# Gathered expert rows taken earlier in a two-layer step, with the slots, the one-hot chunks and one key search moved in the hand-written order

## The chip, the cores and the metric

The kernel runs on one core of a Trainium2 chip, as one launch. The metric is the device time of one execution in microseconds (us), less is better. The engines are TensorE (PE in the profile, PEld for its weight loads), VectorE (DVE), ScalarE (ACT), GpSimd (POOL) and the issuing engine SyncE (SP).

## The reference, cut to what matters

The step has DEPTH = 2 layers over 128 prompt tokens (tile 0) and 512 latent tokens (tiles 1 to 4). Each layer has an attention and gating part and then PEER, a retrieval of experts, which is where the changed code lies:

```python
q = (x @ w_q).reshape(n, PEER_HEADS, 2, PEER_HALF)          # 8 heads
s1 = jnp.einsum('nhd,kd->nhk', q[:, :, 0], key1)            # 128 keys each
s2 = jnp.einsum('nhd,kd->nhk', q[:, :, 1], key2)
t1, i1 = lax.top_k(s1, 16); t2, i2 = lax.top_k(s2, 16)
cand = t1[..., :, None] + t2[..., None, :]
top, pos = lax.top_k(cand.reshape(n, 8, 256), 16)           # 128 experts a token
g = jax.nn.softmax(top, axis=-1)
a = jnp.einsum('thkd,td->thk', u_tab[ib], xb)
w = jax.nn.gelu(a) * gb
out = jnp.einsum('thk,thkd->td', w, v_tab[ib])              # tables of 16384 x 1024
```

Everything is float32.

## The kernel before, in words

**Two ways to do the experts.** A token needs 128 rows of `peer_u` and 128 of `peer_v`. A tile can be *gathered*: POOL issues one indirect DMA for each of 128 slots (each brings one row of 1024 numbers for each of the 128 tokens, 512 KB), DVE multiplies and sums (`dot_rows`, line 1313, for u; `add_rows`, line 1331, for v). Or it can be *dense*: PE multiplies by the whole table, 128 blocks of 128 experts, and most products get a weight of zero. Tiles 0 and 2 are gathered in both halves, tiles 3 and 4 are dense in both, and tile 1 is gathered for u and dense for v (`GATHERED`, `U_DENSE`, `V_DENSE`). "A row" below is one such slot of a tile, written u0, v0, u1, u2, v2 by table and tile; each of the five has 128.

**The stages of a layer.** First the *front*, once for the prompt (g = "P") and once for the latent tiles (g = "S"): input projection, attention, output projection, query projection with the scores of the keys, and the first tile's key search. Then the *u pass* (line 942): PE runs 128 blocks, each 8 matmuls (16 instructions in the profile) over 256 tokens. Then the *v pass* (line 970): 128 blocks of 12 instructions, each over 512 columns, for three tiles. `u_order` writes the order of PE and ACT in the u pass by hand. Between the blocks stand, for each tile k of `V_DENSE` = [3, 4, 1], one slot job `slT` (line 947: the chosen experts' numbers and weights are transposed) after the block that `SLOT_BLOCKS` names, and then 32 chunks `g` (line 954), after the blocks that `chunk_block` names. A chunk turns one-hot vectors of four tokens into their gate weights over all experts.

**DVE has one order of its own**, written out at the end of `build`: the searches (`choosing(k, i)`: i = 0 to 15 are the sixteen half-key searches, done in pairs on odd i; i = 16 to 21 combine them), the one-hots of a chunk (`one_hots`, lines 1499 and 1504, at most 5 chunks ahead of PE), and rows between them. `slots_out(k)` tells PE that slT may run; `one_hots(k, 0)` waits until ACT has emptied slT's bank. Then comes the v pass, where `weights_T(b)` (line 1514) makes the weights of block b, at most four blocks ahead of PE, with the rows of tiles 0 and 2 between. Blocks up to `LAST_U` have the last v0 rows and the rest of tile 2's search, then `finish_gathered(0)`; those up to `LAST_V` have the u2 rows, those up to `LAST_END` the v2 rows.

**Rows come through a ring of GP = 8 buffers.** POOL issues them in the order of `ROWS` (line 681) as DVE releases buffers, so a row that DVE takes later is also loaded later. In the front, DVE takes u0 rows with `prompt_rows(n)`: some before the attention, one or two beside each of its 32 heads, 8 after it, some before and beside the queries; `expert_weights(0)` then needs the Gelu of ACT over all 128 dots (`gelu_dots(0)`, which waits for the last u0 row), and `add_rows(0, ...)` begins.

**SP and ACT issue the other transfers**: SP the blocks of both tables (two blocks a DMA, four DMAs ahead), the stores of the u pass's activations and half of the gate stores, and their loads in the v pass (`load_gates`, `load_acts`); ACT the other half of the gate stores. ACT also runs in order, and waits in it for DVE at `top_softmax(k)` and `gelu_dots(k)`, which stand at written blocks.

## Time and profile before

| | |
|---|---|
| median of 3 runs | 3688.99 us (3688.4 to 3696.15) |
| the profiled execution's own time | 3688.44 us |
| its span in the profile | 3686.3 us |
| PE busy | 3445.9 us (93%) |
| DVE busy | 2621.7 us (71%) |
| ACT busy, POOL busy | 861.4 us (23%), 1602.0 us (43%) |
| moved by DMA | 1263.48 MB, mean 343 GB/s |
| mean granted TensorE clock | 0.966 |

The page gives busy times over the whole span, and PE looks full. The matmul ends are modelled, though, so for PE the number of instructions in a stretch beside its length says more than the busy time. The two layers are alike, and a layer's stages have different limits, so a stretch has to be read by itself.

### The profile page before, as it was taken

The page shows a single profiled execution, that of the slowest core. Times are in us where ns is not written, and L with a number is a line of the kernel's source. Part 1 is how long each engine was busy: PE and PEld are TensorE (multiplying, and loading weights), DVE is VectorE, ACT ScalarE, POOL GpSimd, SP SyncE. Part 2 cuts the span into 40 slices and gives each one's busy share as a digit, 9 for nine tenths or more (in the row PEclk, how much of TensorE's full clock was granted, in tenths as well). Part 3 has the DMA queues.
Part 4 walks back from the last instruction along what each step waited for, and adds up shares of the span by engine and source line. Part 5 has one row for each costly group of instructions (what it writes and reads, how often), then busy time and mean ns, then how long its engine had stood idle before and what let it go on. Part 6 is the DMA issues. An engine that isn't in the chain of part 4 may idle for free.

```text
span 3686.3 us, 38219 instructions
## 1 busy us (share of the span) xinstructions
PE 3445.9 (93%) x12478; PEld 2100.3 (57%) x12478; DVE 2621.7 (71%) x6009; ACT 861.4 (23%) x2206; POOL 1602.0 (43%) x1362
## 2 busy tenths in 40 slices
PE   6898989999799999999988988999998999999998
PEld 2555446889687444444435554488986864444443
DVE  0377786978788766666645786789787886666667
ACT  1115211158632000000021260111685210000000
POOL 2044265424642555555400542645156235555552
PEclk9898999999999999999989989999998999999999
DMA  9866588999999999999974864899899999999994
GB/s 361 331 241 218 181 322 328 380 325 345 409 406 367 397 384 414 414 413 413 374 268 151 311 202 173 329 365 402 292 386 409 397 357 386 414 414 413 414 413 193
DMA packets 413988, 1263.48 MB, mean 343 GB/s; under 512 B 36240, under 2 KB 139664, under 8 KB 370784
## 3 DMA queue, kind: packets, MB, share of 16 engines
q0 software_dynamic: 192000, 721.61, 50.5%
q1 hardware_dynamic: 171808, 514.20, 36.8%
q10 hardware_dynamic: 49984, 25.23, 2.3%
q8 instruction: 101, 1.65, 0.2%
q14 instruction: 95, 0.78, 0.1%
HBM read 1174.07 MB, written 86.84 MB: 342 GB/s over the span
## 4 chain that ended last, share of the span: by engine, by line
PE 52%; DMA 27%; DVE 8%; issue 5%; POOL 4%; ACT 2%; SPq 1%; ACTq 0%; DVEq 0%; POOLq 0%
PE P L942 21%; DMA ring<-in_peer_v_dram,eidx 12%; DMA ring<-in_peer_u_dram,eidx 10%; PE P L916 8%; POOL ring L681 4%; PE T L954 4%; PE P L750 4%; PE P L767 4%; DMA ring<-in_w_mod_dram 2%; PE P L970 2%; PE O L814 2%; PE T L750 2%; DMA gate_d<-area 1%; DVE ring L1313 1%; DVE late L1331 1%
## 5 line engine op out<-in xcount | busy, mean ns | idle before, releaser
L681 POOL DMA_INDIRECT ring<-in_peer_u_dram,eidx x768 | 947.1, 1233 | 1139.6 <-DVE ring L1313 785.9
L1313 DVE SCALAR_TENSOR_TENSOR ring<-ring,h 128x1024 f32<-128x1024 f32 x768 | 925.0, 1223 | 296.9 <-DMA ring<-in_peer_u_dram,eidx 289.8
L970 PE MATMUL P<-w_ring,area 128*128 128x512 f32 x2048 | 927.3, 596 | 33.9 <-DVE area L1514 32.4
L942 PE MATMUL P<-hT,w_ring 128*128 128x256 f32 x4096 | 921.1, 383 | 0.0
L681 POOL DMA_INDIRECT ring<-in_peer_v_dram,eidx x512 | 615.1, 1201 | 671.7 <-DVE late L1331 347.0
L942 PEld LDWEIGHTS P<-hT,w_ring 128*128 128x128 f32 x4096 | 778.4, 193 | 102.8
L970 PEld LDWEIGHTS P<-w_ring,area 128*128 128x128 f32 x2048 | 388.7, 191 | 535.2 <-issue 535.2
L1331 DVE SCALAR_TENSOR_TENSOR h<-ring,dots,h 128x1024 f32<-128x1024 f32 x254 | 325.9, 1283 | 184.5 <-DMA ring<-in_peer_v_dram,eidx 175.8
L1331 DVE SCALAR_TENSOR_TENSOR late<-ring,dots,late 128x1024 f32<-128x1024 f32 x254 | 325.8, 1283 | 71.3 <-DMA ring<-in_peer_v_dram,eidx 56.3
L916 PE MATMUL P<-hT,w_ring 128*128 128x128 f32 (+1 forms) x1024 | 286.4, 441 | 2.9 <-issue 2.9
L970 PE MATMUL O<-w_ring,qT 128*128 128x512 f32 x512 | 261.4, 592 | 0.0
L970 PE MATMUL V<-w_ring,qT 128*128 128x512 f32 x512 | 261.4, 592 | 0.0
L916 PEld LDWEIGHTS P<-hT,w_ring 128*128 128x128 f32 x1024 | 158.2, 195 | 127.1 <-issue 122.7
L1199 ACT ACTIVATE qT<-hT 128x128 f32<-128x128 f32 x128 | 39.3, 309 | 625.6 <-PE V L970 625.6
L1199 ACT ACTIVATE qT<-area 128x128 f32<-128x128 f32 x128 | 38.9, 309 | 586.6 <-PE V L970 586.6
L970 PEld LDWEIGHTS O<-w_ring,qT 128*128 128x128 f32 x512 | 97.3, 190 | 122.7 <-issue 122.7
L970 PEld LDWEIGHTS V<-w_ring,qT 128*128 128x128 f32 x512 | 97.3, 190 | 122.5 <-issue 122.5
L954 PE MATMUL T<-row 128*128 128x128 f32 x912 | 126.4, 287 | 35.4 <-issue 33.9
L954 PEld LDWEIGHTS T<-row 128*128 128x128 f32 x912 | 120.6, 200 | 45.5 <-issue 39.1
L750 PE MATMUL P<-w_ring,hT 128*128 128x512 f32 x320 | 142.2, 604 | 3.0 <-ACT hT L1088 3.0
L767 PE MATMUL P<-w_ring,hT 128*128 128x512 f32 x320 | 139.1, 593 | 1.5 <-issue 1.5
L647 POOL DMA_DIRECT2D ring<-in_w_mod_dram x48 | 25.8, 540 | 207.2 <-PE O L717 146.8
(233 smaller groups left out, 3205.0 us busy)
## 6 DMA issues: line engine op xcount, KB each, us to landing
w_ring<-in_peer_uT_dram SPq DMA_DIRECT2D x128, 1024.0 KB, 8.3
w_ring<-in_peer_vB_dram SPq DMA_DIRECT2D x128, 1024.0 KB, 8.2
ring<-in_w_mod_dram POOLq DMA_DIRECT2D x48, 1024.0 KB, 8.3
w_ring<-in_peer_wq_dram SPq DMA_DIRECT2D x64, 512.0 KB, 5.8
h<-acts_d SPq DMA_DIRECT2D x64, 512.0 KB, 9.0
w_ring<-in_w_in_dram SPq DMA_DIRECT2D x48, 512.0 KB, 5.0
area<-gate_d SPq DMA_DIRECT2D x16, 1536.0 KB, 14.2
hT<-gate_d SPq DMA_DIRECT2D x16, 1536.0 KB, 14.4
```

The lines of the kernel that those rows point to most:

```text
L647: pool.dma_start(m_slots[:, u % MR], chunks(w_mod)[ml, :, c, n * MW:(n + 1) * MW]).then_inc(m_full[u % MR], 16)
L681: pool.indirect_dma_start(out=ring[:, b, :], out_offset=None, in_=tables["uv".index(phase)], in_offset=bass.IndirectOffsetOnAxis(ap=eidx[: ...
L750: mm = pe.matmul(out[:, 0:width], hT[:, c, t * P:(t + 1) * P], w[:, c % 2, 0:width], start=c == 0, stop=c == DC - 1)
L767: mm = pe.matmul(out[:, :], hT[:, c, t * P:(t + 1) * P], w_ring[:, ws[4 * n + q], c % 2, :], start=c == 0, stop=c == DC - 1)
L814: mm = pe.matmul(out[:, :], v_pad[:, kb, HD * kv:HD * kv + P], pT[:, kv, i, :], start=kv == 0 and i == 0, stop=kv == 1 and i == len(keyb) - 1)
L916: mm = pe.matmul(out[:, 0:nt * P], w[:, c % 2, j * P:(j + 1) * P], hT[:, c, 0:nt * P], start=c == 0, stop=c == DC - 1)
L942: mm = pe.matmul(out[:, 0:TOKENS], w[:, c * P:(c + 1) * P], hT[:, c, TOKENS:2 * TOKENS], start=c == 0, stop=c == DC - 1)
L954: mm = pe.matmul(out[:, j * P:(j + 1) * P], oh_b[n % OH_BUFS][:, j, :], oh_a[n % OH_BUFS][:, j, :], start=True, stop=True)
L970: mm = pe.matmul(bank[ACC[2 * t + half]][:, :], w, uv_ring[:, b // 2 % (WR // 2), b % 2, half * 512:(half + 1) * 512], start=b == 0, stop= ...
L1199: act.activation(wdot_T[:, b % 4, :].rearrange("p (s t) -> p s t", t=SUB), gate_in[b // 8 % 2][:, ACT_SUBS:SUBS, b % 8, :], ACT.Copy).then ...
L1313: dve.scalar_tensor_tensor(ring[:, b, :], ring[:, b, :], 1.0, h2[:, k, :], ALU.mult, ALU.mult, accum_out=dots[:, k, row:row + 1]).then_inc ...
L1331: dve.scalar_tensor_tensor(acc[k], ring[:, b, :], dots[:, k, row:row + 1], acc[k], ALU.mult, ALU.add).then_inc(row_used[b], 1)
```

## The change

It keeps every operation and every byte, and changes only where they stand in the order. In the front of the latent tiles, 36 u0 rows instead of 28 stand before the attention, two after each of the first three tiles of the output projection, 18 instead of 24 before the queries, 20 instead of 28 beside the first queries. ACT's Gelu of the dots comes at query 7 instead of 10, and 52 v0 rows instead of 40 lie beside queries 7 to 15. In the u pass the first search (tile 3) has 20 v0 rows (24 before) and 16 u1 rows, the search of tile 4 has 32 u1 rows (16 before), the chunks of tile 4 have 62 u1 rows (78 before) and the sixteen half-key searches of tile 2, which stood at the end of the pass; the chunks of tile 1 have 28 v0 rows (16 before). Slots come after blocks 43, 75 and 101 (50, 78 and 103 before), chunks from block 47, 77 and 103 (52, 80 and 105). In the v pass 28 v0 rows are left (48 before), tile 2's u rows lie at blocks 14 to 69 (20 to 70), its v rows at 70 to 122 (71 to 122).

```diff
-PV_EARLY = 64
-PV_LATE = 80
+PV_EARLY = 72
+IN_ROWS = 36
+OUT_ROWS = 2
+QUERY_ROWS = 52
+PV_LATE = 100
...
-LAST_U = 20
-LAST_V = 71
+LAST_U = 14
+LAST_V = 70
...
-SLOT_BLOCKS = {50: 3, 78: 4, 103: 1}
+SLOT_BLOCKS = {43: 3, 75: 4, 101: 1}
 
 SEARCH_CHUNKS = 22
 
+ROWS_BESIDE = 32
...
     if k == 3:
-        return 52 + q if q < SEARCH_CHUNKS else 73 + (q - SEARCH_CHUNKS) // 2
-    first, blocks = {4: (80, 23), 1: (105, 16)}[k]
+        return 47 + q if q < SEARCH_CHUNKS else 70 + (q - SEARCH_CHUNKS) // 2
+    first, blocks = {4: (77, 23), 1: (103, 16)}[k]
...
-                        if g == "S" and j == 10:
+                        if g == "S" and j == 7:
                             gelu_dots(0)
...
-                        if b == 43:
+                        if b == 41:
                             top_softmax(3)
-                        if b == 68:
+                        if b == 65:
                             top_softmax(4)
-                        if b == 102:
+                        if b == 100:
                             gelu_dots(1)
...
                     if latent:
-                        prompt_rows(28)
+                        prompt_rows(IN_ROWS)
...
                         norm_modulate(g, t)
+                        if latent and t < nt - 1:
+                            prompt_rows(OUT_ROWS)
                     if latent:
-                        prompt_rows(SLOTS - 28 - 40 - GP - 28)
+                        prompt_rows(SLOTS - IN_ROWS - 40 - GP - OUT_ROWS * (nt - 1) - 20)
                     modulation("summed")
                     for j in range(2 * PH):
-                        if latent and j < 8:
-                            prompt_rows(3 + j % 2)
-                        if latent and j == 10:
+                        if latent and j < 5:
+                            prompt_rows(4)
+                        if latent and j == 7:
                             expert_weights(0)
-                        if latent and j >= 10:
-                            add_rows(0, 40 * (j - 10) // 6, 40 * (j - 9) // 6)
+                        if latent and j >= 7:
+                            add_rows(0, QUERY_ROWS * (j - 7) // 9, QUERY_ROWS * (j - 6) // 9)
                         first_tile_keys(g, j)
...
                 for i in range(2 * PH + 6):
                     if i < 12:
-                        add_rows(0, 40 + 2 * i, 42 + 2 * i)
+                        add_rows(0, QUERY_ROWS + (PV_EARLY - QUERY_ROWS) * i // 12,
+                                 QUERY_ROWS + (PV_EARLY - QUERY_ROWS) * (i + 1) // 12)
...
                 for i in range(2 * PH + 6):
-                    dot_rows(1, 16 + 16 * i // 22, 16 + 16 * (i + 1) // 22)
+                    dot_rows(1, 16 + ROWS_BESIDE * i // 22, 16 + ROWS_BESIDE * (i + 1) // 22)
                     one_hots(3, i)
                     choosing(4, i)
...
-                    dot_rows(1, 32 + i, 33 + i)
-                dot_rows(1, 42, 50)
+                    dot_rows(1, 16 + ROWS_BESIDE + i, 17 + ROWS_BESIDE + i)
+                near = 16 + ROWS_BESIDE + CHUNKS - SEARCH_CHUNKS + GP
+                dot_rows(1, near - GP, near)
                 for i in range(CHUNKS):
                     one_hots(4, i)
-                    dot_rows(1, 50 + 78 * i // CHUNKS, 50 + 78 * (i + 1) // CHUNKS)
+                    dot_rows(1, near + (SLOTS - near) * i // CHUNKS, near + (SLOTS - near) * (i + 1) // CHUNKS)
+                    if i % 2:
+                        choosing(2, i // 2)
                 slots_out(1)
                 for i in range(CHUNKS):
                     one_hots(1, i)
-                    add_rows(0, PV_EARLY + i // 2, PV_EARLY + (i + 1) // 2)
-
-                for i in range(SEARCHED_EARLY):
-                    choosing(2, i)
+                    add_rows(0, PV_EARLY + (PV_LATE - PV_EARLY) * i // CHUNKS,
+                             PV_EARLY + (PV_LATE - PV_EARLY) * (i + 1) // CHUNKS)
+
                 for b in range(KEYS):
                     weights_T(b)
```

## Rows read from the trace of the kernel before

**Rows 1.** The page: PE's busy time, and GB/s in 40 slices of the span

```profile
PE 3445.9 (93%) x12478; PEld 2100.3 (57%) x12478; DVE 2621.7 (71%) x6009; ACT 861.4 (23%) x2206; POOL 1602.0 (43%) x1362
GB/s 361 331 241 218 181 322 328 380 325 345 409 406 367 397 384 414 414 413 413 374 268 151 311 202 173 329 365 402 292 386 409 397 357 386 414 414 413 414 413 193
```

**Rows 2.** Busy time by stretch, layer 0: length, engines (instructions), clock, DMA share, GB/s

```profile
603.90:780.50 176.60, 176.60 (x822) 155.47 (x821) 145.70 (x422) 25.86 (x59) 78.43 (x65) 1.00 0.97 381
780.50:905.70 125.20, 125.05 (x701) 113.21 (x701) 108.51 (x352) 99.31 (x257) 37.57 (x33) 1.00 0.93 317
905.70:1062.00 156.30, 129.81 (x668) 113.40 (x667) 121.84 (x224) 96.05 (x253) 98.13 (x80) 0.92 1.04 408
1062.00:1175.50 113.50, 111.89 (x642) 101.30 (x641) 94.82 (x309) 27.79 (x61) 19.45 (x18) 1.00 1.03 371
```

**Rows 3.** The same by pass: u and v of layer 0, v of layer 1

```profile
603.90:1175.50 571.60, 543.35 (x2827) 483.39 (x2826) 470.88 (x1307) 249.01 (x628) 233.58 (x194) 0.98 0.99 372
1175.50:1855.00 679.50, 665.37 (x1535) 291.57 (x1536) 464.13 (x706) 41.77 (x131) 354.56 (x303) 0.99 0.99 396
...
2987.60:3669.90 682.30, 663.97 (x1535) 291.61 (x1536) 468.08 (x713) 41.81 (x131) 357.75 (x296) 0.99 0.96 386
```

**Rows 4.** The chain that ended last, in order of time: start, us, what

```profile
402.93 27.47 PE P L767 x64
...
604.04 176.12 PE P L942 x816
...
804.78 0.89 PE T L954 x8
```

**Rows 5.** DMA issues by line: KB each, median us to landing

```profile
w_ring<-in_peer_uT_dram SPq DMA_DIRECT2D x128, 1024.0 KB, 8.3
...
acts_d<-late SPq DMA_DIRECT2D x64, 256.0 KB, 9.9
gate_d<-area ACTq DMA_DIRECT2D x32, 512.0 KB, 13.3
```

**Rows 6.** Waits of PE, and of DVE, between 905 and 1062 us

```profile
PE T L954 <- issue: 26.3, 14, 3.9
...
DVE ring L1313 <- DMA ring<-in_peer_u_dram,eidx: 30.8, 31, 2.7
```

**Rows 7.** Groups of DVE instructions, 907 to 1059 and 1062 to 1141 us

```profile
L1313 DVE SCALAR_TENSOR_TENSOR ring<-ring,h 128x1024 f32<-128x1024 f32 x77 | 93.5, 1222 | 31.4 <-DMA ring<-in_peer_u_dram,eidx 30.3
...
L1331 DVE SCALAR_TENSOR_TENSOR late<-ring,dots,late 128x1024 f32<-128x1024 f32 x16 | 20.4, 1274 | 0.0
```

**Rows 8.** DVE's timeline at the entry of the latent attention, layer 0

```profile
246.48 1.23 DVE L1313 SCALAR_TENSOR_TENSOR ring<-ring,h 128x1024 f32<-128x1024 f32 x1 [0.55 <-DMA ring<-in_peer_u_dram,eidx]
...
278.45 0.61 DVE L1616 CUSTOM_DVE_ANT_0 probs<-P,mask,sink 128x384 f32<-128x384 f32 x1
...
287.55 0.69 DVE L1578 BATCH_NORM_STATS2 stats<-area 128x6 f32<-128x512 f32 x1 [4.22 <-ACT area L1014]
...
296.17 1.22 DVE L1313 SCALAR_TENSOR_TENSOR ring<-ring,h 128x1024 f32<-128x1024 f32 x1
```

**Rows 9.** DVE's timeline in the output projection

```profile
430.51 0.69 DVE L1645 TENSOR_TENSOR tmp<-P,area 128x512 f32<-128x512 f32 x1 [2.03 <-PE P L767]
```

**Rows 10.** DVE's waits between 472 and 604 us

```profile
DVE best L1340 <- ACT key_ring L1127: 22.4, 4, 10.6
```

**Rows 11.** DVE's timeline: one pair of half-key searches between rows

```profile
616.15 0.48 DVE L1340 MAX8 best<-key_ring 128x8 f32<-128x128 f32 x2
...
618.62 8.23 DVE L1331 SCALAR_TENSOR_TENSOR late<-ring,dots,late 128x1024 f32<-128x1024 f32 x6
```

**Rows 12.** DVE's timeline: end of tile 1's search, first one-hots of tile 3

```profile
670.87 0.23 DVE L1450 TENSOR_SCALAR eidx<-tmp 128x128 uint32<-128x128 f32 x1
...
781.22 0.69 DVE L1499 TENSOR_TENSOR h<-qT,cst 128x512 f32<-128x512 f32 x1 [13.78 <-ACT qT L1170]
```

**Rows 13.** PE's timeline after `finish_gathered(0)`

```profile
1293.30 6.70 PE L970 MATMUL P<-w_ring,area 128*128 128x512 f32 x8 [6.08 <-DVE area L1514]
```

## The prediction, on record before the changed kernel was built

> **What bounds the kernel now.** I read the page first. It has PE busy for 93% of the span, and it has the transfers near one ceiling, 406 to 414 GB/s, in most slices of the two passes [rows 1]. Neither says which of the two ends a stage, so I went to the stages.
>
> The chain of waits gives what PE needs when nothing holds it: 51 blocks of the u pass in 176.12 us, 3.454 us a block; a chunk in 0.89 us; and 64 instructions over 512 columns in 27.47 us, 0.4292 us each, so 12 x 0.4292 = 5.15 us for a block of the v pass [rows 4]. The u pass needs 128 x 3.454 + 96 x 0.887 = 527 us and took 571.6: **44 us of stall**. The v pass needs 659.4 us and took 679.5 in layer 0 and 682.3 in layer 1: **20 and 23 us** [rows 3]. Nothing else in these two passes can be won, and the fronts, 1181 us or so of the span for both layers, hold the rest.
>
> The stretches of the u pass show where the 44 us lie [rows 2]. Up to 780.5 and 905.7 us PE runs at its floor while the transfers leave room (381 and 317 GB/s). From 905.7 to 1062 us they are full at 408 GB/s, and PE does 25 blocks and 32 chunks, 114.8 us of work, in 156.3 us: 41.5 of the 44. There DVE waited 30.8 us for u rows and PE 26.3 us in 14 waits before chunks [rows 6]. The rest is the clock, granted at 0.92 of 2.4 GHz there and at 1.00 in the stretch before. So 78 rows, packed between the chunks of tile 4, are too many for the transfers, DVE comes late with the one-hots, and PE waits.
>
> **The change, part by part.** A row moves 128 x 1024 x 4 = 0.524 MB, a u block 0.524, its activations 0.131, a chunk's gates 0.262 MB [rows 5, 7]. Positions below are for layer 0 in the times of the old trace; layer 1 repeats them.
>
> *Projection, +8 rows.* DVE took 19 rows in 246.48 to 278.45, 1.68 us each, as it waited for them to land; eight more are 13.4 us. It has cover: after three heads it waited for ACT's Gelu until 287.55 [rows 8], and further between tiles. But ACT's Gelu stands behind the first two heads' Exp, so it moves with DVE: heads at 291.9, Gelu done about 299, the statistics' end at 302.3 in place of 296.17. From there the heads run through DVE, ACT and PE in turn, and I see nothing that catches up. **+6.0 us** a layer; the ends are 0 (all absorbed by waits between tiles) and +13.4.
>
> *Output projection, +6 rows.* Two rows are 2.3 us, and in each tile DVE waits for the second half of PE's product, 2.0 us in the smallest case [rows 9]; before the queries there are 6 rows fewer. 0; without that cover 3 x 2.3 = 7 us.
>
> *Queries.* From the last LayerNorm on DVE has 18 + 20 + 52 = 90 rows, before 24 + 28 + 40 = 92. It still waits for the keys' copies (22.4 us before [rows 10]), but fewer rows are left where the u pass begins and its blocks load beside them. My estimate: 2 rows are 2.6 us, and as much again from those that needn't land in that crowd, so tile 1's search ends near 665 us instead of 670.87 [rows 12]; the ends are 659 and 675 (four rows more in that part, five more us of waits). ACT's Gelu of the dots at query 7 needs row u0 127: 38 rows at 1.22 to 1.68 us and two pair searches, 51 to 69 us [rows 7, 8, 11], against two groups of queries of 27.47 us and their keys, some 61 us. 0 to +8 us; I take 0, since these rows wait in the ring when the part begins and the ring refills during each search.
>
> *First slots.* DVE had finished tile 3's slots 13.78 us before ACT emptied them [rows 12]. The new place is 7 blocks, 24.2 us, earlier: 603.9 + 44 x 3.454 = 755.9 us. DVE started this part 6 us earlier and has 36 instead of 40 rows in it (-5 us): 767.4 - 6 - 5 = 756.4. It fits to a microsecond, and each microsecond that DVE is later is one that PE waits.
>
> *Search of tile 4, up to its slots.* 32 blocks and 32 chunks are 138.9 us of PE. 50 rows, blocks, activations and gates are 55.6 MB, 400 GB/s: just under the ceiling. So slots 4 at 895 us, against 905.7, with three blocks fewer done.
>
> *Chunks of tile 4.* 26 blocks and 32 chunks are 118.2 us of PE. Transfers: 17.0 + 8.4 + 62 x 0.524 = 57.9 MB; the same count gives 65.7 for the old stretch, which moved 408 x 156.3 = 63.8, so I take off 2 to 3.5: 54.4 / 0.408 = 134 us. DVE was busy 121.84 us [rows 2]; 16 rows less at 1.22 and eight pair searches at 2.47 more [rows 7, 11] leave 122. So 134 us, transfers still the limit: the stall falls from 41.5 to 16.
>
> *Chunks of tile 1 and the end.* 26 blocks and 32 chunks, 118.2 us. DVE was busy 94.82 us there [rows 2]; 12 v0 rows more are 15.3 and the searches gone 19.8 us. The last chunk comes two blocks earlier, so the last gate store, on which SP's loads for the v pass wait, has more cover. No stall.
>
> Sum for the u pass: 152 + 139 + 134 + 118.2 + 4 for slots and gaps = 547; I add 5 because two stretches now run within 3% of the transfers' ceiling and DVE meets its first slot without reserve: 552 us, **-19.5 us**. The ends: 0 (bytes of the pass unchanged, and if its stretches don't level out nothing is won) and -26 (no allowance, and less at the ceiling).
>
> *V pass.* It loses 20 rows: 304 were left and 284 are. It moved 396 x 679.5 = 269 MB; now 258.6, 392 GB/s at PE's floor. Blocks 2 to 19 had 48 rows, 2.67 each; now blocks 2 to 13 have 28, 2.33. That matters at `finish_gathered(0)`: DVE came to it without lead and PE waited 6.08 us, then ran 8 instructions at twice their time, +3.4 us [rows 13]. DVE's work from block 2 falls from 3.85 to 3.45 us a block beside the search, against PE's 5.15; the search's 22 us are in both. I expect the 9.5 us gone, and half of the other 11 us, since the u2 rows thin out from 2.51 to 2.29 a block but v2 rows only from 2.46 to 2.42: **-12.5 us** (0 to -18).
>
> Nothing of the kernel's end moves. Sum: 2 x (6.0 - 19.5 - 12.5) = -52. Of this I keep -49, since the first layer's and the second's front can each lose the microsecond or two of ACT's Gelu: 3688.4 - 49 = **3639 us**, against the profiled execution's own 3688.44, which stands 0.5 us under the median 3688.99 and so can be set for it.
>
> **The rivals.** *A, the deadlines win.* DVE misses the earlier slot. It decides if DVE comes to tile 3's slots at or after 767 us in old times, that is, if the query part gives nothing back. For it: the forecast has no reserve there, and the slots moved 24 us while DVE had 13.8. The price: 11 us at the first slots, 5 at tile 4's, DVE and transfers in series in tile 4's chunks (122 busy + 28 of waits as before = 150 instead of 134 us), so the u pass takes 552 + 11 + 5 + 16 = 584, +12 us; with +6 in the front and -8 in the v pass that is +10 a layer: **3708 us**. Against it: the rows before the slots become fewer. *B, half.* The stretch at 400 GB/s stalls too, u pass -9, v pass -9, front +7: -11 a layer, **3666 us**. For it: at 408 GB/s PE stalled in the old trace, and the step from 400 is small. *C, more.* The attention absorbs the late start between its tiles, and the passes reach their floors: 0 - 25 - 17 = -42 a layer, **3605 us**. *D, nothing.* The transfers can't be held above the u pass's mean: its 372 x 571.6 = 212.6 MB take 571 us again, wherever they stand, and the front's +6 meets -6 in the v pass: **3688 us**. Against it: 408 GB/s over 156 us, and 396 over the v pass [rows 2, 3]. The Trainium skill ("DMA: Bandwidth & Descriptors", "Where 436 GB/s comes from") says that between HBM and SBUF the memory's share of a core, about 358 GB/s, binds; by it the u pass would need 594 us and filling light stretches would win nothing. The rows just named lie above that figure, so the trace doesn't agree.
>
> **How the numbers follow.** Forecast 0.50 (its own range 3624 to 3655), A 0.09, B 0.23, C 0.12, D 0.06. The range reaches into B, D and C: 3612 to 3684. Faster by over 0.2% (7 us, about what a measurement can tell from no change): forecast, B, C and the upper part of D, 0.86. Within: 0.05. Slower: 0.09.
>
> **What the profile would show.** Right: the statistics of the latent attention end about 6 us later after its start; DVE's wait at tile 3's first one-hots is a few us instead of 13.8; the stretch of tile 4's search moves 380 to 400 GB/s instead of 317; PE's waits before chunks fall from 26 to some 10 us; the u pass takes 546 to 558 us; PE doesn't wait for line 1514 after `finish_gathered(0)`; the v pass takes 665 to 670 us. Wrong: PE idle before tile 3's slots, ACT waiting for DVE at `gelu_dots(0)` with PE behind it, or a u pass still above 565 us.

## The result, and the profile after

The changed kernel takes **3666.17 us** in the median of 4 runs (3659.94 to 3672.84); the kernel before, run beside it, 3689.59 us (3688.4 to 3696.15). The ratio is 0.993, with the 95% interval 0.9917 to 0.9944. A second set of runs gave it 3653.24 us against 3692.92, ratio 0.9886 (0.9872 to 0.9901). So it is faster by 0.7 to 1.1%, inside the range given and 27 us (in the second set 14) above the forecast of 3639. The two sets' intervals don't overlap, so a difference of some 10 us between kernels of different sets says little. The profiled execution took 3659.94 us, with a span of 3658.1, 28.2 less than before; the second set's profile has the same span.

The page of the changed kernel, the lines that answer to [rows 1]:

```profile
PE 3434.4 (94%) x12478; PEld 2101.6 (57%) x12478; DVE 2617.4 (72%) x6009; ACT 860.4 (24%) x2206; POOL 1728.9 (47%) x1362
...
GB/s 361 329 225 264 197 308 326 379 370 370 408 387 377 390 414 413 399 414 412 333 273 153 340 205 194 306 390 375 360 382 408 349 383 401 413 414 398 413 415 170
```

The transfers are more level, as intended, and PE is as full as it was. The page says no more. (Lines of the changed kernel are 5 higher than before: 942 is 947, 1313 is 1318, 1514 is 1519, and so on; x2 and x4 add 2, e3 adds 1.) The changed kernel by stretch, in the columns of [rows 2]: the u pass of layer 0 cut at the Gelus of blocks 43, 75 and 101, then the v passes of both layers.

```profile
610.80:762.80 152.00, 152.00 (x705) 133.47 (x703) 136.87 (x412) 23.10 (x52) 69.24 (x58) 1.00 0.98 386
762.80:908.20 145.40, 141.29 (x775) 127.67 (x775) 130.69 (x392) 101.96 (x262) 68.88 (x51) 0.99 1.00 365
908.20:1058.70 150.50, 127.11 (x678) 112.49 (x677) 120.03 (x320) 93.58 (x254) 82.93 (x65) 0.94 1.05 406
1058.70:1178.10 119.40, 118.67 (x676) 107.61 (x674) 86.75 (x191) 30.27 (x63) 56.11 (x28) 1.00 1.01 369
1178.10:1838.90 660.80, 659.30 (x1536) 291.53 (x1537) 443.54 (x688) 42.18 (x131) 363.29 (x283) 1.00 0.98 392
...
2982.60:3641.80 659.20, 659.14 (x1535) 291.56 (x1536) 445.49 (x692) 42.23 (x131) 357.72 (x276) 1.00 0.95 383
```

[Rows 2] were cut where the kernel before has its stages. For a like comparison the kernel before is cut at the same blocks, 43 to 75 to 101 to 127:

```profile
756.00:893.20 137.20, 137.12 (x744) 123.55 (x744) 110.33 (x353) 96.73 (x247) 33.19 (x30) 1.00 0.91 310
893.20:1051.80 158.60, 132.93 (x687) 116.44 (x685) 122.68 (x223) 101.95 (x269) 102.70 (x81) 0.92 1.04 408
1051.80:1175.50 123.70, 121.20 (x692) 109.48 (x692) 103.36 (x327) 30.28 (x66) 24.98 (x23) 1.00 1.03 374
```

From here A is blocks 0 to 43, B 44 to 75, C 76 to 101 with the chunks of tile 4, D 102 to 127 with the chunks of tile 1 (in the old placement the slots and chunks stand a few blocks later). With [rows 4] the changed kernel's PE needs 152, 138.9, 118.2 and 118.2 us in them, and 659.4 us in the v pass; the shortest that any run with this placement shows are 139.4 us for B and 119.4 for D. Every profile, cut so:

```
us                layer 0:  A     B     C     D     v     u    layer 1:  B     C     D     v     u
before                    152.1 137.1 158.7 123.7 679.5 571.6          137.1 158.8 123.1 682.3 571.2
after                     152.1 145.3 150.5 119.4 660.8 567.3          147.9 151.4 125.3 659.2 576.6
after, second set         152.1 147.7 150.7 119.4 658.8 569.9          147.5 151.0 119.4 659.7 570.0
e1 old slots, chunks      152.1 137.1 158.1 124.1 660.6 571.4          137.1 158.5 124.0 659.5 571.7
e2 28 rows first          152.1 145.4 150.8 119.4 658.8 567.7          147.9 150.8 119.4 659.7 570.2
e3 half of a u block      152.1 139.4 137.8 119.4 658.8 548.7          139.4 138.3 119.4 659.7 549.2
e4 gates stored early     152.1 144.1 150.2 119.4 658.8 565.8          148.5 149.2 119.4 659.5 569.2
e5 16 rows back into C    152.1 148.4 161.8 122.9 660.9 585.2          147.6 163.3 120.0 661.0 582.9
e6 20 v0 rows back        152.1 148.5 150.6 119.4 677.5 570.6          141.5 150.7 119.5 679.7 563.8
e7 before, gates early    152.1 137.1 159.6 128.8 677.3 577.7          137.1 159.8 127.8 680.9 576.9
e8 before, new front      152.1 137.1 158.8 123.6 679.2 571.7          137.1 158.8 124.7 683.6 572.7
x1 slots 2 blocks later   152.1 139.4 149.7 126.2 658.8 567.4          139.4 148.2 126.2 659.7 565.9
x2 v0 rows held back      152.1 145.0 149.7 122.2 658.8 569.1          141.4 150.1 120.1 659.6 563.6
x4 x2 and e4              152.1 147.6 144.2 119.9 660.5 563.8          145.7 145.3 119.4 659.7 562.6
```

The 28.2 us of span split into -16.2 in layer 0 (fronts +6.8, u pass -4.3, v pass -18.7) and -12 in layer 1 (+5.8, +5.4, -23.1). **The v pass brought all of it, and more; the u pass, meant to bring most, brought little.** The second set's profile has it 1.7 and 1.2 us shorter than before.

*V pass.* It is at PE's floor. Before, in layer 0, PE waited 14.1 us in 14 waits for the weights of line 1514. In the changed kernel there are two short waits for them (line 1519 now). DVE, which before had waited 197 us for rows in this pass and never for PE's blocks, now waits 56 us for rows and 139.5 us for PE to catch up, four blocks behind it. Then DVE's timeline around `finish_gathered(0)`, which answers to [rows 13]; PE doesn't stop there:

```profile
PE P L975 <- DVE area L1519: 2.2, 2, 1.5
...
DVE area L1519 <- PE V L975: 139.5, 83, 4.7
```

```profile
1245.45 1.22 DVE L1310 TENSOR_TENSOR late<-late,h 128x1024 f32<-128x1024 f32 x1
...
1254.27 1.22 DVE L1318 SCALAR_TENSOR_TENSOR ring<-ring,h 128x1024 f32<-128x1024 f32 x1
```

*Front.* DVE's timeline in layer 0: entry of the latent attention and the first row after the statistics there, against [rows 8]; end of tile 1's search, tile 3's slots ready, and first one-hots of tile 3, against [rows 12]. Then PE's first use of tile 3's slots.

```profile
293.32 0.61 DVE L1621 CUSTOM_DVE_ANT_0 probs<-P,mask,sink 128x384 f32<-128x384 f32 x1
...
305.36 1.22 DVE L1318 SCALAR_TENSOR_TENSOR ring<-ring,h 128x1024 f32<-128x1024 f32 x1
...
679.10 0.23 DVE L1455 TENSOR_SCALAR eidx<-tmp 128x128 uint32<-128x128 f32 x1
...
766.42 0.29 DVE L1448 TENSOR_TENSOR gsm<-gsm,gsum 128x128 f32<-128x128 f32 x1
...
768.52 0.69 DVE L1504 TENSOR_TENSOR h<-qT,cst 128x512 f32<-128x512 f32 x1 [0.42 <-ACT qT L1175]
```

```profile
766.92 0.66 PE L952 MATMUL O<-ident,r 128*128 128x128 f32 x2 [4.11 <-DVEq L1491]
```

The attention begins 14.9 us later and its statistics end 9.2 us later (305.36 against 296.17). Of both, 3.4 us already stand ahead of the changed code, where tile 0's search ends at 215.2 us instead of 211.8. Counted from there the statistics end 5.8 us later, and 7.4 in layer 1, about as forecast, and the latent front up to the u pass is 3.4 and 6.5 us longer. But tile 1's search ends 68.3 us after the u pass begins (610.8), not earlier than before (67.0 after 603.9). DVE still waits for the keys' copies:

```profile
DVE best L1345 <- ACT key_ring L1132: 24.8, 2, 16.4
```

*Stretch B.* PE's only wait in it, and the 3.4 us behind that wait:

```profile
PE O L952 <- DVEq L1491: 4.1, 1, 4.1
```

```profile
766.90:770.30 3.40, 3.38 (x10) 2.86 (x11) 2.98 (x5) 2.41 (x7) 2.77 (x2) 0.52 0.92 309
```

PE waits 4.1 us for tile 3's slots, and then runs at a granted clock of 0.52, near the lower level of 1.2 GHz. Its busy time in B is 141.3 us against 139.4 in a run without that wait (x1 below). So 4.1 and 1.9 make the 6 us by which B is over that. In layer 1 the wait is 5.6 us and B 147.9: 8.5 over, 5.6 and 2.9. No transfer holds PE up in B, and DVE waits there 0.8 us for rows.

*Stretch C.* Waits of the changed kernel between 908.2 and 1058.7 us (who, for whom: sum, count, longest). [Rows 6] had DVE waiting for rows, and PE before chunks without a releaser that the profile names; a chunk can wait for its one-hots.

```profile
ACT area L1190 <- DMA gate_d<-area: 24.2, 3, 9.4
DVE dots L1295 <- ACT dots L1079: 18.1, 1, 18.1
...
PE T L959 <- ACT area L1190: 11.7, 5, 7.1
...
ACT hT L1190 <- DMA gate_d<-hT: 11.2, 2, 6.1
...
PE T L959 <- ACT hT L1190: 7.7, 3, 4.9
DVE ring L1318 <- DMA ring<-in_peer_u_dram,eidx: 7.5, 7, 1.9
...
PE T L959 <- issue: 3.9, 1, 3.9
```

Now PE waits for ACT to empty a chunk's bank, and ACT for the gate stores to land and give their buffers back. DVE's waits for rows are down from 30.8 to 7.5 us, and at the end of C DVE stands 18.1 us ahead, waiting for ACT's Gelu of tile 1's dots. The forecast had foreseen the fall in DVE's waits, not ACT's part. PE's three waits sum to 23.3 of the 32.3 us by which C is over 118.2; the other 9 are PE busy for 127.1 us, at a granted clock of 0.94 in the stretch.

### The profile page after: what moved, and what is told of

Read it like the earlier page. It is cut to its first block, busy times and chain, and to the rows that moved or that the text cites. A ratio compares the mean times of both kernels' runs of the same rounds, so it can differ in the third digit from the quotient of the medians.

```text
span 3658.1 us, 38233 instructions
## 1 busy us (share of the span) xinstructions
PE 3434.4 (94%) x12478; PEld 2101.6 (57%) x12478; DVE 2617.4 (72%) x6009; ACT 860.4 (24%) x2206; POOL 1728.9 (47%) x1362
## 4 chain that ended last, share of the span: by engine, by line
PE 66%; DVE 14%; DMA 11%; issue 3%; POOL 2%; ACT 2%; SPq 1%; ACTq 0%; DVEq 0%; POOLq 0%
PE P L975 23%; PE P L947 10%; PE P L921 6%; PE V L975 6%; PE O L975 6%; DVE late L1336 4%; PE P L772 4%; DMA gate_d<-hT 3%; PE T L959 3%; POOL ring L686 2%; PE P L755 2%; DMA ring<-in_w_mod_dram 2%; DMA ring<-in_peer_v_dram,eidx 2%; PE O L819 2%; DMA acts_d<-late 1%
## 5 line engine op out<-in xcount | busy, mean ns | idle before, releaser
L686 POOL DMA_INDIRECT ring<-in_peer_u_dram,eidx x768 | 984.3, 1282 | 1011.9 <-DVE ring L1318 644.4
L686 POOL DMA_INDIRECT ring<-in_peer_v_dram,eidx x512 | 704.7, 1376 | 621.1 <-DVE late L1336 348.4
L1336 DVE SCALAR_TENSOR_TENSOR late<-ring,dots,late 128x1024 f32<-128x1024 f32 x254 | 329.1, 1296 | 55.6 <-DMA ring<-in_peer_v_dram,eidx 38.5
L1519 DVE TENSOR_TENSOR area<-h,area 128x256 f32<-128x256 f32 x128 | 54.0, 425 | 194.2 <-PE V L975 136.7
L1519 DVE TENSOR_TENSOR area<-h,hT 128x256 f32<-128x256 f32 x128 | 54.4, 425 | 143.4 <-PE V L975 143.1
L755 PE MATMUL P<-w_ring,hT 128*128 128x512 f32 x320 | 141.5, 602 | 3.0 <-ACT hT L1093 3.0
```

The lines of the kernel that those rows point to most:

```text
L686: pool.indirect_dma_start(out=ring[:, b, :], out_offset=None, in_=tables["uv".index(phase)], in_offset=bass.IndirectOffsetOnAxis(ap=eidx[: ...
L755: mm = pe.matmul(out[:, 0:width], hT[:, c, t * P:(t + 1) * P], w[:, c % 2, 0:width], start=c == 0, stop=c == DC - 1)
L1336: dve.scalar_tensor_tensor(acc[k], ring[:, b, :], dots[:, k, row:row + 1], acc[k], ALU.mult, ALU.add).then_inc(row_used[b], 1)
L1519: dve.tensor_tensor(wexp_T[:, b % 4, :].rearrange("p (s t) -> p s t", t=SUB), act_in[:, b // 4 % 2, b % 4, :].rearrange("p (s t) -> p s t" ...
```

## The experiments

The question was where the u pass's expected 19.5 us went. One theory: its transfers' total sets the u pass, wherever they stand. The other: single waits do (the slots in B, the stores or the rows in C).

**Rows of the last stretch back into the v pass.**

```diff
-PV_LATE = 100
-LAST_U = 14
-LAST_V = 70
+PV_LATE = 80
+LAST_U = 20
+LAST_V = 71
```

> The changed kernel with v0 rows 80 to 127 left to the v pass as before (48 rows there, 8 beside tile 1's chunks), and LAST_U and LAST_V at their old 20 and 71; so 20 rows go from the u pass back to the v pass. Theory 1 (both passes are bound by the time of their transfers, 1.27 us a row): the u passes take 542 to 552 us instead of 567, the v passes 674 to 682 instead of 660, and the kernel 3655 to 3680, within 15 us of the changed one. The prediction's reasoning (only tile 4's chunks are too full; the room is elsewhere): u pass 560 to 567, v pass 674 to 682, kernel 3690 or more.

3691.42 us (3686.28 to 3704.59) against 3692.92, ratio 0.9998 (0.9989 to 1.0007). The profile of e6: stretch D, v pass of layer 0, v pass of layer 1, then PE's wait for the weights.

```profile
1064.10:1183.50 119.40, 118.68 (x675) 107.61 (x674) 66.19 (x173) 30.22 (x63) 9.85 (x9) 1.00 0.87 285
1183.50:1861.00 677.50, 663.49 (x1535) 291.30 (x1536) 464.05 (x706) 41.80 (x131) 352.88 (x303) 0.99 0.99 397
...
2992.60:3672.20 679.60, 664.22 (x1535) 291.81 (x1536) 468.38 (x713) 41.71 (x130) 357.79 (x296) 0.99 0.96 387
```

```profile
PE P L975 <- DVE area L1519: 14.0, 12, 6.1
```

Those 20 rows, with the two marks that follow from them, hold the whole gain: without them in D the changed kernel is the old one in time. They take 18.7 and 20.0 us out of the v passes (against the second set's) and cost D nothing: it takes 119.4 us at a DMA share of 0.87 and at 1.01. The theory of the total falls, since the u pass does not shorten by the 20 rows' 10.5 MB, 26 us at 408 GB/s. In layer 1 it is 6 us shorter, all in B, ahead of where the rows were: there PE waits only 1.9 us for tile 3's slots, and the clock stays at 1.00. B follows that wait in every profile with the new placement: 1.7 us in x2's layer 1 (B 141.4), 7.0 in e6's layer 0 (148.5).

**The front's part alone, on the kernel before.**

```diff
-                        prompt_rows(28)
+                        prompt_rows(36)
...
+                        if latent and t < nt - 1:
+                            prompt_rows(2)
...
-                        if latent and j == 10:
+                        if latent and j == 7:
                             expert_weights(0)
...
-                        add_rows(0, 40 + 2 * i, 42 + 2 * i)
+                        add_rows(0, 52 + i, 53 + i)
```

> The kernel before with the change's front alone (36 rows, two after each tile, the queries' rows and Gelu at query 7), and 12 v0 rows instead of 24 beside the first search; slots, chunks, the search of tile 2 and all later rows as before. DVE begins the u pass some 12 to 15 rows ahead. Theory 1: the u passes are shorter by those rows' time, 12 to 17 us, the v passes stay 675 to 682, the front costs 3 to 6: kernel 3665 to 3680, most of the change's gain. The prediction's reasoning: the first stretch had room already, tile 4's chunks are as full as before, so the u pass stays 567 to 571 and the kernel is 6 to 12 us slower than before, 3695 to 3705.

3706.75 us (3700.59 to 3715.2) against 3692.92, ratio 1.0038 (1.0024 to 1.0052). The profile of e8, stretches B and C:

```profile
764.10:901.20 137.10, 137.03 (x744) 123.47 (x743) 99.85 (x340) 96.66 (x246) 27.62 (x25) 1.00 0.86 288
901.20:1060.10 158.90, 133.26 (x688) 116.55 (x686) 123.00 (x226) 102.32 (x270) 104.08 (x82) 0.92 1.04 408
```

The front alone costs 13.8 us in the medians, 6.9 a layer (6.3 and 6.7 in the profiles, counted from the end of tile 0's search), and gives the u pass nothing by itself: B's load falls from 310 to 288 GB/s, and C stays as it was. It is a price paid for room that only the rest of the change fills.

**Fewer rows ahead of the attention, on the changed kernel.**

```diff
-IN_ROWS = 36
+IN_ROWS = 28
```

> 28 u0 rows before the attention as before the change, so eight more stand before the queries (26). The prediction's step: the statistics of the latent attention end 6 us sooner, in each layer. If those 6 us reach the end, the kernel takes 3654, 12 less than the changed one; but eight rows later in the query part push DVE's first slot 5 to 10 us further behind PE (4.3 and 5.8 us of stall there now). Theory 1 lets that stall be made good by transfers later, so 3654 to 3660; if DVE's date at the first slot binds by itself, no gain, 3664 to 3670.

3656.77 us (3654.44 to 3657.95) against 3693.07, ratio 0.9905 (0.9889 to 0.9922). Counted from the end of tile 0's search the statistics end 5.8 and 7.4 us earlier, yet the latent front, from tile 0's search to the u pass, takes 398.8 and 395.0 us against 395.8 and 397.8. Part of what is saved ahead of the attention comes back at the queries: in layer 0 ACT waits 4.8 us for row u0 127, and PE 6.3 us for ACT behind it in place of 1.5. So the front's price doesn't hang on these eight rows alone.

**Slots, chunks and marks at their old blocks.**

```diff
-SLOT_BLOCKS = {43: 3, 75: 4, 101: 1}
+SLOT_BLOCKS = {50: 3, 78: 4, 103: 1}
...
-        return 47 + q if q < SEARCH_CHUNKS else 70 + (q - SEARCH_CHUNKS) // 2
-    first, blocks = {4: (77, 23), 1: (103, 16)}[k]
+        return 52 + q if q < SEARCH_CHUNKS else 73 + (q - SEARCH_CHUNKS) // 2
+    first, blocks = {4: (80, 23), 1: (105, 16)}[k]
```

> The changed kernel with slots, chunks and ACT's waits back at their old blocks (50, 78, 103); all rows and searches as changed. If the placement was what the u pass gained (the prediction's reasoning), the pass is 10 us longer or more and the kernel above 3685. Theory 1: the same bytes move at the same share, so within 5 us a layer of the changed kernel; PE's 4.3 and 5.8 us before the first slot vanish, and the last gate stores, later now, may give 2 to 4 us back before the v pass. Kernel 3660 to 3675.

3659.82 us (3657.78 to 3661.05) against 3693.07, ratio 0.991 (0.9894 to 0.9927); the interval overlaps the changed kernel's. The profile of e1, stretch C and two waits in it:

```profile
902.10:1060.30 158.20, 130.64 (x690) 115.99 (x690) 134.37 (x345) 100.49 (x270) 97.83 (x74) 0.92 1.05 408
```

```profile
ACT hT L1190 <- DMA gate_d<-hT: 28.2, 3, 11.6
...
ACT area L1190 <- DMA gate_d<-area: 15.7, 5, 8.5
```

The old placement gives the old times to a microsecond, 137.1, 158.1 and 124.1, though the order has 16 rows fewer between tile 4's chunks than the old one (the packets of C hold 75.8 rows against 76.9, as the ring loads ahead). What the new placement takes from C and D it gives back in B. And C is as long with ACT waiting 44 us for its gate stores as it was with DVE waiting for rows.

**Half of the bytes of a u block.** It leaves out half of the columns of each block that SP loads, so the dense products of tiles 3 and 4 are half old data; PE's work is the same.

```diff
-                    sp.dma_start(uv_ring[:, i % (WR // 2)], peer_uT[l, i])
+                    sp.dma_start(uv_ring[:, i % (WR // 2), :, 0:D // 2], peer_uT[l, i][:, :, 0:D // 2])
```

> Leaves out half of the columns of every u block that is loaded (33.5 MB a layer less to move; PE, ACT and DVE do the same instructions, on stale numbers in that half). Theory 1, the u pass is bound by the time of its transfers (the share of the 16 engines is 0.97 to 1.05 in every stretch of it after the change, although the rate is only 367 to 406 GB/s): the pass of layer 0 falls from 567 us to 530 to 537, near PE's 527, and ACT's waits for gate stores all but vanish. Theory 2, the gate stores' three staging places turn round too slowly because SP issues its half of a store two to three blocks late, whatever the load: the stores still cost PE 10 us or more in tile 4's chunks and the pass stays above 545 us. Theory 3, DVE's dates (first slots too early): 4.3 us are left at the first slot in either case.

A single run, 3618.08 us. The profile of e3, stretch C:

```profile
901.00:1038.80 137.80, 125.24 (x678) 111.96 (x677) 119.08 (x320) 93.86 (x254) 81.96 (x64) 0.95 1.04 399
```

B falls to 139.4, PE's need, and C to 137.8 and 138.3, still 20 over the 118.2. In B the transfers act through A: DVE's waits for v0 rows before tile 3's slots fall from 10.5 to 0.4 us, it comes to the slots in time, and PE's wait there is gone. In C 6.3 MB less (54.9 against 61.2) are 16 us at 400 GB/s, and C gave 12.7, so transfers set part of its excess, and something is left that these bytes don't pay for.

**Sixteen rows back beside tile 4's chunks.**

```diff
-ROWS_BESIDE = 32
+ROWS_BESIDE = 16
```

> The changed kernel with 16 u1 rows beside tile 4's search as before, so 78 instead of 62 between its chunks; slots and chunks as changed. Theory 4: blocks 44 to 75 come back from 146 us to 142 to 143 (PE's 138.9 and the wait before the first slots), blocks 76 to 101 go from 150.5 up by 16 rows less the 8 that no longer fit in as refill, to 158 to 168; u pass 575 to 582, kernel 10 to 25 us slower than the changed one. Rival 5: no row count matters there, within 4 us of the changed kernel.

3682.9 us (3675.47 to 3687.25) against 3690.49, ratio 0.9967 (0.9955 to 0.998). The profile of e5, stretch C and PE's largest wait in it:

```profile
916.50:1078.30 161.80, 133.50 (x677) 116.89 (x676) 140.76 (x352) 96.65 (x254) 103.70 (x81) 0.92 1.04 408
```

```profile
PE T L959 <- issue: 28.3, 14, 6.4
```

C is 11.3 and 11.9 us longer for 16 rows, 0.73 us each, and PE's waits with no releaser named return. B keeps its 148, with PE waiting 6.7 and 5.3 us at the slots: B's excess is not made by the rows moved into it.

**The first slots two blocks later.** Slots of tile 3 after block 45, of tile 1 after 103, with their chunks and marks.

```diff
-SLOT_BLOCKS = {43: 3, 75: 4, 101: 1}
+SLOT_BLOCKS = {45: 3, 75: 4, 103: 1}
...
-        return 47 + q if q < SEARCH_CHUNKS else 70 + (q - SEARCH_CHUNKS) // 2
-    first, blocks = {4: (77, 23), 1: (103, 16)}[k]
+        return 48 + q if q < SEARCH_CHUNKS else 70 + (q - SEARCH_CHUNKS) // 2
+    first, blocks = {4: (77, 25), 1: (105, 14)}[k]
```

> The changed kernel with the first slots at block 45 and the last at 103, 25 blocks instead of 23 for tile 4's chunks and 14 instead of 16 for tile 1's. Theory 4: the same bytes lie over two more blocks, so PE's stall in them shrinks by up to the 6.9 us of PE's work that they add less 3.2 us for these blocks' own bytes; the 4.3 to 5.8 us before the first slots go, the last chunk still comes before the end. Kernel 4 to 14 us faster than the changed one. If the last gate store is then too late for the v pass, 4 to 8 us a layer come back before it.

3655.51 us (3651.37 to 3657.22) against 3690.49, ratio 0.9893 (0.9871 to 0.9915): no gain beside the changed kernel. The profile of x1, stretches B and D:

```profile
768.50:907.90 139.40, 139.40 (x773) 126.08 (x773) 127.79 (x389) 100.25 (x261) 67.00 (x50) 1.00 1.00 371
...
1057.60:1183.80 126.20, 122.55 (x684) 109.44 (x682) 88.88 (x194) 30.74 (x64) 32.33 (x29) 1.00 1.02 362
```

B is at PE's need in both layers, without a wait of PE and with the clock at 1.00: the 6 to 8.5 us over it were the wait at the slots and the lower clock behind it. It reaches this at 371 GB/s and a DMA share of 1.00, so such a share holds nothing up by itself. D is 6.8 longer: tile 1's chunks lie in 14 blocks in place of 16 and start two later, PE waits 3.0 us for their one-hots, and one chunk more falls behind the cut. This run moved both places, and so doesn't give what the first alone would.

**Gate stores of SP one DMA of blocks earlier**, on the changed kernel and on the one before.

```diff
-    return [part for part, b in enumerate(ends) if (b + 9) // 2 == i]
+    return [part for part, b in enumerate(ends) if (b + 7) // 2 == i]
```

> SP issues its half of every gate store one pair of blocks sooner, nothing else. Theory 2 (turnround of the staging places): ACT's waits for gate stores in tile 4's chunks, 35 us in layer 0, fall by 7 us or more for each of some five waits, the u pass by 10 to 20 us, the kernel by 20 to 40. Theory 1 (time of the transfers): the wait moves to another place, the u pass stays within 4 us of 567, the kernel within 8 us of 3666.

> The kernel before with SP's half of the gate stores one pair of blocks sooner. In it PE waited for DVE's one-hots and not for stores. Theory 2 (turnround of staging): no gain where the stores were not waited for, kernel 3684 to 3696. Theory 1: the same. If it gains 10 us or more, the sooner stores help by something else than the wait for staging, and what that is stays open.

On the changed kernel 3645.4 us (3640.41 to 3650.19) against 3693.07, ratio 0.9878 (0.9861 to 0.9894); on the one before 3700.25 (3695.29 to 3706.45) against 3692.92, ratio 1.0018 (1.0008 to 1.0028). The changed kernel with this edit is 13 us below the least that the transfers' theory allowed (3658), but the changed kernel by itself is 5 below it in the next set (see there). The profile of e4, stretch C and waits in it:

```profile
904.50:1054.70 150.20, 129.97 (x678) 115.82 (x676) 120.06 (x320) 94.21 (x253) 82.45 (x64) 0.91 1.05 408
```

```profile
ACT late L1157 <- DMA acts_d<-late: 20.6, 3, 9.2
...
PE T L959 <- ACT area L1190: 9.7, 2, 5.3
ACT k_sb L1157 <- DMA acts_d<-k_sb: 9.1, 1, 9.1
```

ACT's waits for gate stores are gone, and in their place it waits for activation stores, which share SP's queue: C stays at 150. One wait changed its name. On the kernel before D grows to 128.8 and 127.8 us: in layer 0 ACT waits 11.7 us for an activation store, tile 1's slots come late, and PE waits 5.4 us for them.

**Tile 0's v rows held back until tile 1's slots are out**, so that the ring isn't filled with them in C; then this with the early gate stores.

```diff
                 for phase, k, lo, hi in ROWS:
...
+                    if (phase, k, lo) == ("v", 0, PV_EARLY):
+                        pool.wait_ge(slots_ready, (l + 1) * len(V_DENSE))
```

> The changed kernel, but POOL waits for the last slots (tile 1's) before it issues v0 row 72, so that the ring isn't refilled with v0 rows while tile 4's chunks run. Theory 4 (the stretch of tile 4's chunks, blocks 76 to 101, is bound by what is moved in it at 406 GB/s: 61.0 MB in 150.5 us with 68 rows, of which 62 are u1 and the rest this refill; the stretch of tile 1's chunks stands at PE's floor and has room): that stretch falls by 6 rows, 3.1 MB, to 142 to 144 us, the next one stays 119 to 122, the kernel gains 10 to 16 us on the changed one. Rival 5 (this stretch is bound by the order and landing time of the stores, not by how much is moved): it stays 149 to 152 and nothing is gained.

> Both edits of the two earlier kernels on the changed one: no refill before the last slots, and SP's half of the gate stores one pair of blocks sooner. Alone each left blocks 76 to 101 at 149 to 150 us. If the stretch is bound twice, by what is moved and by how late a store is issued, so that each edit only uncovers the other bound, both together take it to 140 to 145 us and the kernel to 3625 to 3640. If it is bound by how fast DVE draws the 62 u1 rows in its first 120 us (share 1.046 there whatever is edited), it stays 147 to 151 and the kernel takes 3640 to 3655, as the sooner stores alone.

x2: 3654.58 us (3653.21 to 3663.72) against 3690.49, ratio 0.99 (0.9882 to 0.9918). x4: 3647.21 (3642.23 to 3655.52) against 3694.69, ratio 0.9876 (0.9858 to 0.9894). Stretch C in the profile of x2, and in that of x4:

```profile
910.10:1059.80 149.70, 129.34 (x678) 114.90 (x677) 119.93 (x320) 93.75 (x254) 71.72 (x58) 0.92 1.02 390
```

```profile
914.60:1058.80 144.20, 126.46 (x677) 113.07 (x676) 119.96 (x320) 94.22 (x253) 73.58 (x58) 0.93 1.05 404
```

Each alone leaves C at about 150, though x2 has 7 rows fewer in it (58 against 65 of POOL's instructions); both together give 144.2 and 145.3. So two things bind C at once, what is moved and when a store's buffer is back, and only both together shorten it. 144 is still 26 over PE's need: 17.7 us of waits and 8.3 of longer work at a granted clock of 0.93. Three lines of x4's waits in C:

```profile
ACT late L1159 <- DMA acts_d<-late: 17.0, 3, 9.1
...
PE T L961 <- ACT area L1192: 7.0, 2, 6.0
...
PE P L949 <- DMA w_ring<-in_peer_uT_dram: 4.9, 1, 4.9
```

ACT still waits for activation stores, and PE now waits once for a block of the table itself.

**The changed kernel again**, in the set of e6 to e8.

> The changed kernel once more, word for word, as the measure for the others of this job. All theories: 3655 to 3675, and the u pass of layer 1, 576.6 us in its first profile, nearer to layer 0's 567.3.

3653.24 us (3646.22 to 3659.88) against 3692.92, ratio 0.9886 (0.9872 to 0.9901). Its profile repeats A, C and the v passes within 2 us; D of layer 1 took 125.3 in the first profile, with one wait of 3.7 us for one-hots, and 119.4 in this one, so the u pass of 576.6 was not the rule. e4 and x4 have the lowest ratios of the study, 0.9878 and 0.9876, but their intervals overlap this one: neither is shown to beat the change.

## Why the prediction was right or wrong

**Right: what bounds the passes** and that only stalls can be won; that the front costs about 6 us a layer (3.4 and 6.5 between the profiles, counted from tile 0's search, 6.9 in e8's medians), with the statistics 5.8 and 7.4 us later for the 6.0 forecast; that fewer rows ahead of `finish_gathered(0)` free PE there; that 12 v0 rows more in D cost nothing (119.4 us, against 118.2). The time fell inside the range, on rival B's 3666 in the first set, but not by B's split of -9, -9 and +7. The number owes something to luck: the v pass gave 6 to 11 us a layer more than forecast and so made up for part of the 15 and 25 that the u pass fell short. Two of the signs named for a wrong forecast were there: PE idle before tile 3's slots, and a u pass of 567 us, above 565; PE's waits before chunks are 23 us in C, not some 10.

**V pass, right in mechanism, too small: -12.5 taken, -18.7 and -23.1 measured**, of 20.1 and 22.9 to be had. The step gave back "half of the other 11 us", since v2 rows thin out only from 2.46 to 2.42 a block. e6 shows that all of PE's waits there go with the 20 rows. A stage whose tightest stretch had 3.85 us of DVE work a block against 5.15 was late from gaps (DVE's 197 us of waits for rows) and not from load, and a lead won early was kept to the end. That this lead is also why the later rows land in time is read from the waits, not tested apart from the 20 rows.

**First slots, wrong: "DVE started this part 6 us earlier".** It didn't: tile 1's search ended 68.3 us after the pass began, where the forecast needed 61. The row taken for cover, DVE's wait for the keys' copies [rows 10], was a wait that stays (24.8 us) whatever rows stand beside it. What came after it up to the slots took 9 us less than before, not 5 (766.7 - 679.1 = 87.6 against 767.4 - 670.9 = 96.5), but this didn't make it up: PE waited 4.1 us and then ran slower for a while, 6 us together, 8.5 in layer 1. The forecast had said that the fit had no reserve; for that, for gaps and for two full stretches it had 4 + 5 us in the sum.

**Search of tile 4, "400 GB/s: just under the ceiling": the term was right (138.9 us; x1 shows 139.4), the fear of the ceiling was not.** The stretch took 145.3 to 147.9 us, and all that it had over is the late first slots. It moved 53.0 MB where the forecast counted 55.6, at 365 GB/s. The DMA share of 1.00 looks like a full one, but the packets show otherwise: in C the 8-KB pieces of blocks run at 423 GB/s and the 4-KB pieces of rows at 411 (bytes over the engines' time, worked out from single packets), in B only at 365 and 391, and in the old B, which moved 310 GB/s, at 321 and 372. Packets took longer in the lighter stretches, so the share of a light stretch reads too high: from the old B to the new the rate rose by 18% and the share by 10%. What makes them longer no run here shows.

**Chunks of tile 4, wrong: "54.4 / 0.408 = 134 us".** This is the step that cost most: the term is 16.5 us short in layer 0 and 17.4 in layer 1. 61.2 MB moved in 150.5 us, 6.8 MB more than the 54.4 of the sum. The term counted 62 rows; the stretch loaded 67.7, as the ring refills with v0 rows before D, 3.0 MB; and "I take off 2 to 3.5" took off bytes that did move. (54.4 / 0.408 is 133.3, not 134.) x2 takes the refill out and gains nothing alone, so the size of the sum doesn't explain the time either: behind the row waits stood the stores' landing, e4's and x4's subject, a wait of ACT that the trace before hid behind the other. The forecast asked what is late next for DVE, and not for ACT; DVE itself ended C 18.1 us early.

**The allowance** of 5 us for two stretches near the ceiling and a first slot without reserve stood against 6 to 9 us in B, all from the slot, and 16 to 17 in C: about a fifth of what came.

**Rivals.** A's mechanism came true and small: DVE was 4 us late at tile 3's slots, and B is 6 to 9 us over its need; but in old times DVE came at 760 us, not at A's 767, and the u pass stayed far from A's 584. D has the u pass's number, 571, nearly right, for a reason that falls: moves that fill light stretches do win, 19 us a layer in the v pass, and e6 refutes its total. The Trainium skill ("DMA: Bandwidth & Descriptors", "Where 436 GB/s comes from") has the memory's share of about 358 GB/s bind between HBM and SBUF; C's 406 and the v pass's 392 GB/s over 660 us lie above it, so no run here agrees. The Trainium skill adds in its section "Measured" that a lone core measures more than with its neighbour streaming, and these runs were on one core.

**Open:** how the rest of C's excess in x4 (activation stores, one late block of the table, waits that the profile names no releaser for) would go; why DVE comes to tile 3's slots 2 to 7 us late in profiles of the same code; what the first slots at block 45 would give without moving tile 1's. That the granted clock fell because of the waits is read from their order in time and was not tested by itself.

## What to carry to other kernels

Look at which wait of PE ends last in a stretch before calling it full: B ran at a DMA share of 1.00 with and without its excess, and only the wait at the slots told the two apart. A deadline that is moved up to where the engine just makes it costs the lateness and the slower clock behind it, here 1.9 us on 4.1. Count what a ring loads ahead for the next stage. A move out of a pass whose engine waits can win all of those waits, if the place it goes to has slack in every resource, as D had (20 rows more for nothing). When one wait is removed, look up who else waits on the same transfers before giving the time away, and test the two together: e4 and x2 show nothing at C that x4 shows.

## What the runs showed of the hardware

Stores in 512-byte pieces ran at 303 GB/s in C (bytes over the engines' time), beside 389 for 2-KB, 411 for 4-KB and 423 for 8-KB pieces. Pieces of 8 KB ran at 321 to 423 GB/s from stretch to stretch, slower in the lighter ones, so equal DMA shares did not mean equal rates: 1.00 went with 365 GB/s in B and 0.98 with 392 in the v pass. With the transfers full, a store's landing came to bind: ACT waited up to 9.4 us at a time for a 512-KB gate store (11.6 in e1) and, where that was relieved, 9.2 for a 256-KB activation store. Behind PE's wait of 4.1 us the granted clock was 0.52 for the next 3.4 us; behind the waits of 1.7 and 1.9 us in layer 1 of x2 and e6 it stayed at 1.00 over stretch B.
